# A transformer layer with retrieved experts on one core: three waits and one merge moved in the order of the engines' work

## The reference

```python
h = rmsnorm(x, g_mix);  z = h @ w_in      # pool channels | q | k | v | gate_pool | gate_attn
pool_branch = pool_mixer(p, pool_w, pool_scale) @ w_pool_out
attn_branch = gqa_attention(rope(norm(q)), rope(norm(k)), v) @ w_attn_out
x = x + (sigmoid(gate_pool) * pool_branch + sigmoid(gate_attn) * attn_branch) @ w_out
x = x + peer(rmsnorm(x, g_ffn), ...)
y = rmsnorm(x, g_final)

def peer(h):                              # for each token, 8 heads
    q = (h @ w_query).reshape(8, 2, 128)
    s = q . sub_keys                      # 2 x 128 scores a head
    sv, si = top_k(s, 16)                 # of each half
    cand = sv[0][:, None] + sv[1][None, :]            # 256 pairs, expert id = si0 * 128 + si1
    top_s, pos = top_k(cand, 16);  gate = softmax(top_s)
    a = h . expert_u[idx]                 # 128 experts a token (8 heads x 16)
    return sum(gelu(a) * gate * expert_v[idx])
```

## Time and profile before

| | before |
|---|---|
| median of 3 runs | 2856.29 us (2851.89 to 2860.07) |
| profiled execution | 2854.17 us, span of the trace 2852.4 us |
| PE busy | 2606.1 us (91%) |
| PE weight loads | 1549.7 us (54%) |
| DVE busy | 2088.7 us (73%) |
| ACT busy | 537.9 us (19%) |
| POOL busy | 1571.6 us (55%) |
| moved by DMA | 996.18 MB, 349 GB/s over the span |
| mean granted TensorE clock | 0.967 |

### The profile page before, as it was taken

One profiled execution on the slowest core, in us unless ns is written; L12 is line 12 of the kernel. 1 busy time (PEld: TensorE's weight loads), 2 busy tenths in 40 slices (PEclk: granted clock), 3 DMA queues, 4 the chain that ended last, 5 costly groups with the idle time before them and its releaser, 6 DMA issues.

```text
span 2852.4 us, 30906 instructions
## 1 busy us (share of the span) xinstructions
PE 2606.1 (91%) x9957; PEld 1549.7 (54%) x9957; DVE 2088.7 (73%) x4622; ACT 537.9 (19%) x1205; POOL 1571.6 (55%) x1284
## 2 busy tenths in 40 slices
PE   7999988989787997999589999899999999999998
PEld 6867867875234474555444455455454545444454
DVE  1232977888608876788889988977777778778786
ACT  2141151211008114544520000110000000100101
POOL 0000166456764774444267777677766667666672
PEclk9999999999999998999899999999999999999999
DMA  7538689988997897999899999999999999999994
GB/s 243 188 130 288 248 295 412 410 309 307 344 369 244 329 408 287 345 332 309 309 351 396 413 382 413 377 394 413 412 413 413 413 413 414 413 413 412 407 412 192
DMA packets 305988, 996.18 MB, mean 349 GB/s; under 512 B 26432, under 2 KB 107200, under 8 KB 276672
## 3 DMA queue, kind: packets, MB, share of 16 engines
q0 software_dynamic: 184320, 671.17, 60.9%
q1 hardware_dynamic: 69664, 292.02, 26.3%
q10 hardware_dynamic: 51872, 31.46, 3.6%
HBM read 932.68 MB, written 61.87 MB: 349 GB/s over the span
## 4 chain that ended last, share of the span: by engine, by line
PE 29%; DVE 27%; DMA 26%; issue 11%; POOL 4%; ACT 2%; another core or an unknown queue 1%; DVEq 0%; ACTq 0%; POOLq 0%; SPq 0%
DMA ring<-in_expert_v,idx 15%; PE bank L699 10%; DMA ring<-in_expert_u,idx 9%; PE bank L687 8%; DVE ring L1416 7%; PE bank L978 3%; POOL ring L1381 3%; PE o_bank L968 2%; PE o_bank L719 2%; DVE consts L1834 2%; DVE h L1416 2%; DVE consts L1828 2%; DVE region_c L1416 2%; PE bank L758 1%; DVE neg_max L1510 1%
## 5 line engine op out<-in xcount | busy, mean ns | idle before, releaser
L1381 POOL DMA_INDIRECT ring<-in_expert_u,idx x468 | 605.6, 1294 | 659.2 <-DVE idx L1719 294.2
L978 PE MATMUL bank<-wslot,gate_attn 128*128 128x512 f32 x1536 | 703.3, 609 | 54.8 <-DVE gate_attn L1768 54.7
L1381 POOL DMA_INDIRECT ring<-in_expert_v,idx x428 | 500.0, 1168 | 335.3 <-issue 113.9
L968 PE MATMUL o_bank<-region_a,wslot 128*128 128x384 f32 x2048 | 681.2, 486 | 0.0
L968 PEld LDWEIGHTS o_bank<-region_a,wslot 128*128 128x128 f32 x2048 | 389.0, 190 | 298.0 <-issue 60.3
L978 PEld LDWEIGHTS bank<-wslot,gate_attn 128*128 128x128 f32 x1536 | 296.2, 195 | 419.3 <-issue 322.8
L1416 DVE CUSTOM_DVE_ANT_0 ring<-ring,h 128x1024 f32<-128x1024 f32 x380 | 451.9, 1222 | 67.7 <-DMA ring<-in_expert_u,idx 65.2
L1433 DVE SCALAR_TENSOR_TENSOR region_b<-ring,dots,region_b 128x1024 f32<-128x1024 f32 x256 | 328.6, 1284 | 127.9 <-DMA ring<-in_expert_v,idx 111.1
L1286 ACT ACTIVATE gate_attn<-o_bank 128x384 f32<-128x384 f32 x128 | 62.7, 490 | 1279.9 <-PE o_bank L968 1270.1
L699 PE MATMUL bank<-region_b,wslot 128*128 128x256 f32 (+1 forms) x768 | 231.6, 460 | 1.6 <-ACT region_b L1015 1.6
L699 PE MATMUL bank<-region_a,wslot 128*128 128x256 f32 (+1 forms) x768 | 228.2, 455 | 1.2 <-ACT region_a L1015 1.2
(11 more groups left out here) (215 smaller groups left out, 2892.1 us busy)
## 6 DMA issues: line engine op xcount, KB each, us to landing
wslot<-in_expert_uT SPq DMA_DIRECT2D x64, 1024.0 KB
wslot<-in_expert_v SPq DMA_DIRECT2D x64, 1024.0 KB
wslot<-kept_weights SPq DMA_DIRECT2D x53, 1024.0 KB
kept_weights<-wslot SPq DMA_DIRECT2D x29, 1024.0 KB, 8.7
expert_weights<-region_p ACTq DMA_DIRECT2D x24, 1024.0 KB
wslot<-in_w_in SPq DMA_DIRECT2D x13, 1024.0 KB
region_p<-expert_weights SPq DMA_DIRECT2D x8, 1536.0 KB
region_s<-expert_weights SPq DMA_DIRECT2D x7, 1536.0 KB
```

The costliest lines, as they stand in the source:

```text
L968: ins = nc.tensor.matmul(dense_in[q][:, 0:DENSE_T], u_cols[slot][:, k, :], mergeds[1][:, k, T - DENSE_T:T], start=(k == 0), stop=(k == KD ...
L978: ins = nc.tensor.matmul(dense_out[2 * t + n][:], hidden[q][:, t * P:(t + 1) * P], v_cols[slot][:, n * 512:(n + 1) * 512], start=start, st ...
L1381: nc.gpsimd.indirect_dma_start(ring_row(n), None, expert_u if what == "u" else expert_v, bass.IndirectOffsetOnAxis(ap=ids, axis=0)).then_i ...
```

## The change

Five things are moved; no arithmetic is added or taken away.

1. SP: before the first column loads (and the reload of h2T ahead of them) it waits for job `("chosen", 2)`, the turned ids and gates of the last dense tile.
2. The fourth part of the first merge (`merge(0, 0)`, heads 6 and 7) leaves the end of group 0's `top_halves`; its steps run two at a time between the `attn_out` steps of group 1. With it, `gate_exp(0)` goes from group 1's attention to after its gates on ACT, `softmax(0)` from group 1's attention to after `norm2(1)` on DVE, and `turn_ids(g, 0)` from before `gate_attn` to after `out` on PE and to after `norm2(1)` on DVE. The dots are dealt anew: 12 become 16 ahead of `pool_out(1)`, 15 become 13 in `attn_out(1)`, 12 become 8 in `out(1)`, 8 become 10 after `norm2(1)`.
3. `out`: the number of dots at each step is a list now, and there are none ahead of the last step. In group 2, 28 become 24.
4. After `norm2(2)` the one-hots of jobs 0 and 1 come first; the last dots of the second tile (19 now, 15 before) and `weigh(1)` come after them, ahead of the one-hots of jobs 2 and 3. On ACT `gelu(1)` goes ahead of the stores of jobs 2 and 3, while `take_weights(1)` stays behind them.
5. Turned weights of the first tile: `turn_weights(2, 0)` on PE and `take_weights(0)` on ACT come after the first pool job instead of before it; the quad that was added after that job is added after the second, which has two.

```diff
@@ -1,3 +1,4 @@
+import itertools
 from contextlib import ExitStack
 
 import concourse.bass as bass
@@ -97,7 +98,7 @@
 SUM_BUFS = 4
 SUM_W = 2 * QUAD_ROWS - 1
 SEGMENTS = (
-    (0, {**{("p", c, tp): 1 for c in range(2) for tp in range(2)}, ("pooled",): 2, ("mixed",): 2,
+    (0, {("p", 0, 1): 2, ("p", 1, 0): 1, ("p", 1, 1): 1, ("pooled",): 2, ("mixed",): 2,
          **{("gate_pool", d): 2 for d in range(KD)}, **{("pool_out", d): 1 for d in range(KD)}}),
     (1, {("query", 0, 2): 1, ("query", 0, 3): 1,
          **{("query", c, step): 1 for c in range(1, KD) for step in range(4) if step != 2 or c in (2, 3, 4, 5, 6)},
@@ -120,6 +121,7 @@
 PIECE = 2
 PIECES = {2: (3, 0), 3: (0, 0), 4: (3, 2), 5: (0, 2), 6: (3, 4)}
 PARTS_AT = {2: 1, 3: 2, 0: 4, 1: 9}
+MERGE_STEPS = 2
 PARTS_SENT = {0: PEER_HEADS // PIECE - 1, EARLY: 2}
 MERGE_AT = {1: (2, PARTS_SENT[EARLY] * PIECE), 9: (3, 0), 26: (4, 0)}
 AGAIN_AT = {3: 3, 5: 4}
@@ -166,8 +168,9 @@
         yield from heads + pool + gates
     elif g == FIRST_GROUP[1]:
         yield from heads
+        yield pool[0]
         yield (g, "wT", 0), None
-        yield from pool + gates
+        yield from pool[1:] + gates
     else:
         yield from gates
     for d in range(KD):
@@ -187,8 +190,6 @@
             yield (g, "s", i + 3), None
         yield (g, "probsT", i), None
         yield (g, "probsT", i + 1), None
-    if g == LAST_GROUP[0]:
-        yield (g, "ids", 0), None
     for c in range(KD // 2):
         for d in (2 * c, 2 * c + 1):
             yield (g, "gate_attn", d), (g, "gate_attn", c)
@@ -200,6 +201,8 @@
     for c in range(D // CHUNK):
         for tp in tile_pairs(g):
             yield (g, "out", c, tp), (g, "out", c)
+    if g == LAST_GROUP[0]:
+        yield (g, "ids", 0), None
     for k in range(KD):
         yield (g, "h2T", k), None
     for c in range(HALVES // 2):
@@ -632,6 +635,7 @@
 
             for c in range(HALVES // 2 - WSLOTS, HALVES // 2):
                 filled(sp, *LAST_JOB[LAST_GROUP[1], "query", c])
+            filled(sp, LAST_GROUP[1], "chosen", len(DENSE) - 1)
             sp.wait_ge(h2t_spilled, 16)
             sp.dma_start(mergeds[1][:, :, T - DENSE_T:T - P], h2t_dram).then_inc(h2t_back, 16)
             for j in range(0, COL_SLOTS, COLS_EACH):
@@ -780,11 +784,11 @@
 
             def project_pool(g):
 
-                if g:
-                    turn_weights(g, 0)
                 for c in range(2):
                     for tp in range(2):
                         token_major((g, "p", c, tp), (g, "p", c), hTs[b], BOTH[tp])
+                        if g and (c, tp) == (0, 0):
+                            turn_weights(g, 0)
                         if g:
                             sum_rows("p", c, tp)
 
@@ -892,9 +896,6 @@
                 if g == FIRST_GROUP[1]:
                     pe.wait_ge(sums_added, 1)
                 attention(g)
-                if g == LAST_GROUP[0]:
-                    turn_ids(g, 0)
-
                 for c in range(KD // 2):
                     for d in (2 * c, 2 * c + 1):
                         feature_major((g, "gate_attn", d), (g, "gate_attn", c), hTs[b], d % 2 * P, KD)
@@ -911,6 +912,8 @@
                 for c in range(D // CHUNK):
                     for tp in tile_pairs(g):
                         token_major((g, "out", c, tp), (g, "out", c), mergeds[b], tp)
+                if g == LAST_GROUP[0]:
+                    turn_ids(g, 0)
 
                 pe.wait_ge(h2_half, TILES_BEFORE[g + 1])
                 for k in range(KD):
@@ -1082,11 +1085,12 @@
                 g = FIRST_GROUP[b]
                 if b:
                     gelu(0)
-                    take_weights(0)
-                    weigh_until(0, SUM_BUFS)
                 for c in range(2):
                     for tp in range(2):
                         move(pool_in[:, 2 * tp:2 * tp + 2, c * CHUNK:(c + 1) * CHUNK], (g, "p", c, tp), view=pair)
+                        if b and (c, tp) == (0, 0):
+                            take_weights(0)
+                            weigh_until(0, SUM_BUFS)
                         if b:
                             weigh_sums("p", c, tp)
                 if b == 0:
@@ -1142,8 +1146,8 @@
                 for i in range(0, n, 2):
                     exp(i)
                     exp(i + 1)
-                    if i == 0 and g:
-                        gate_exp(g - 1)
+                    if i == 0 and g == FIRST_GROUP[1]:
+                        gate_exp(1)
                     for ii in (i, i + 1):
                         if g:
                             moved(act, g, "s", ii)
@@ -1189,12 +1193,13 @@
 
                 def stores(c, step):
                     if g == LAST_GROUP[1]:
+                        if (c, step) == TURN_AFTER:
+                            gelu(1)
                         for n in early_weights(c, step):
                             store_weights(n)
                             if n + 2 < 2 * JOBS_PER_TILE:
                                 scale_one_hots(n + 2)
                         if (c, step) == TURN_AFTER:
-                            gelu(1)
                             take_weights(1)
                             weigh_until(1, SUM_BUFS)
                         weigh_sums("query", c, step)
@@ -1310,6 +1315,8 @@
                     gate_exp(2)
                     gate_exp(3)
                 gates(g)
+                if g == LAST_GROUP[0]:
+                    gate_exp(0)
                 if g == LAST_GROUP[1]:
                     take_chosen(0)
                 norm2(g)
@@ -1528,8 +1535,8 @@
                 for i in range(0, n, 2):
                     invert_sum(g, i)
                     invert_sum(g, i + 1)
-                    if i == 0 and g:
-                        softmax(g - 1)
+                    if i == 0 and g == FIRST_GROUP[1]:
+                        softmax(1)
                     dot(rows)
                     if i + 2 < n:
                         row_max(g, i + 2)
@@ -1547,12 +1554,12 @@
                 moved(dve, g, "attn_out", d)
                 nc.vector.tensor_tensor(merged[:, d, cols], merged[:, d, cols], a, ALU.add).then_inc(merged_ready, 1)
 
-            def attn_out(g, rows=KD * (0,)):
-                if g == LAST_GROUP[0]:
-                    turn_ids(g, 0)
+            def attn_out(g, rows=KD * (0,), piece=iter(())):
                 for d in range(KD):
                     attn_out_step(g, d)
                     dot(rows[d])
+                    for _ in zip(range(MERGE_STEPS), piece):
+                        pass
 
             def zero_sums(part):
 
@@ -1579,9 +1586,9 @@
                         if (c, tp) != (D // CHUNK - 1, tile_pairs(g)[-1]):
                             yield
 
-            def out(g, rows=0):
-                for _ in out_steps(g):
-                    dot(rows)
+            def out(g, rows=()):
+                for _, count in itertools.zip_longest(out_steps(g), rows, fillvalue=0):
+                    dot(count)
 
             def norm2(g):
                 b, tiles = GROUP_OF[g]
@@ -1871,19 +1878,24 @@
             norm2(0)
             for hp in range(HALVES):
                 top_halves(0, hp)
-                if hp % (2 * PIECE) == 2 * PIECE - 1:
+                if hp % (2 * PIECE) == 2 * PIECE - 1 and hp < HALVES - 1:
                     merge(0, 0, first=hp // 2 + 1 - PIECE, last=hp // 2 + 1)
 
-            dot(12)
+            dot(16)
             pool_out(1)
             attention(1, 1)
             dot(6)
-            attn_out(1, (3, 3, 3, 2, 2, 2, 0, 0))
+            piece = merge_steps(0, 0, PEER_HEADS - PIECE, PEER_HEADS, fine=True)
+            attn_out(1, (3, 2, 2, 2, 2, 2, 0, 0), piece)
+            for _ in piece:
+                pass
             zero_sums(0)
             dot(6)
-            out(1, 4)
+            out(1, (4, 4, 0))
             norm2(1)
-            dot(8)
+            turn_ids(1, 0)
+            softmax(0)
+            dot(10)
             for hp in range(HALVES):
                 top_halves(1, hp)
                 dot(2)
@@ -1907,16 +1919,16 @@
             zero_sums(1)
             turn_ids(2, 1)
             dot(4)
-            out(2, 4)
+            out(2, (4, 4, 4, 4, 4, 4, 0))
             norm2(2)
-            dot(EARLY * SLOTS - dotted[0])
             piece = iter(())
             for c in range(HALVES // 2):
                 for step_ in range(4):
+                    if (c, step_) == TURN_AFTER:
+                        dot(EARLY * SLOTS - dotted[0])
+                        weigh(1)
                     for n in early_weights(c, step_):
                         one_hots(n)
-                    if (c, step_) == TURN_AFTER:
-                        weigh(1)
                     if c and step_ < 2:
                         top_halves(2, 2 * c - 2 + step_)
                     if step_ == 2 and c in PIECES:
```

## The result

The changed kernel took 2839.39 us (median of 4 runs, 2833.69 to 2840.96), the kernel before 2858.18 beside it (4 runs): ratio 0.9931, 95% interval 0.9905 to 0.9957. Measured again on another chip it was 0.9954 (0.9937 to 0.9970). So 13 to 19 us are gained, where 26 were forecast.

The account below looks back on a forecast made before the run. Column loop bound by full DMA engines, its length fixed; ahead of it PE sets the pace, short of a few waits. 6 + 7.6 - 1.8 + 5.4 + 9.0 = 26.2 us off the 2856.3 median: 2830, range 2816 to 2848.

Parts of the forecast that it names:

- A: Column loads moved behind the last dense tile's turned ids (part 1): late row comes sooner, one-hots at 1371.6, 9.0 us gained.
- C: First tile's turned weights behind the first pool job (part 5): 7.6 us gained, 1.8 given back in fuller transfer stretches.
- (b): Last row of "chosen" stays late, 10 to 12 us, as ACT's store and late rows fill the queue: 2835; chance 0.10.
- (a): Full transfer stretches, 430 to 510 and 630 to 850 us, take B and C back: 2842; chance 0.18.
- B: First merge's part among attn_out steps, fewer dots in out (parts 2 and 3): 7.4 us at h2T, 6 kept.
- (c): Shorter waits also spare slow work at the lower clock, 1.4 to 2 us at four places: 2820; chance 0.13.
- (e): Part 2's steps make DVE late for the gates, out begins 5 to 8 us later: 2850; chance 0.07.
- D: One-hots ahead of the last dots after norm2(2) (part 4): turned weights at 1109.3 instead of 1114.70, 5.4 us gained.
- Its first step: In A, without SP's loads the last "chosen" row takes about 6.2 us instead of 15.03; quad starts at 1366.7.
- The second step: In A, turned ids at about 1369.5 are copied by 1370.4, and the one-hots start at 1371.6, set by DVE.
- The third step: In A, moved loads fall into 1380 to 1440, 13 us of room for 12 needed, costing nothing; without room, 12.
- (d): Slower: stalls like 5.10 us at 1317.85, perhaps engines awaiting instructions, shift onto the path; seven more give 2866; chance 0.05.

Follow-up runs that it names:

- hold_scores: Changed kernel, with GpSimd holding the first row of the second tile (row 256) until group 2's q and k are turned: ratio to before 0.9959.
- paced: Changed kernel, with ten tiny GpSimd fills, not waited for, ahead of each of rows 257 to 268: 2834.84 us, one execution.
- spaced: Changed kernel, with five waited-for GpSimd fills ahead of each of rows 257 to 267 and 509 to 519: ratio to before 0.9982.
- only_d: Kernel before with part 4 alone, out of group 2 keeping its 28 dots, so 15 stand behind the one-hots: ratio 0.9977.
- after again: Changed kernel unaltered, profiled again on another chip: ratio to before 0.9954, median 2834.65 us.
- loads_late: Changed kernel, but SP waits for weight job 84 instead of the last dense tile's turned ids before the first column loads: ratio to before 0.9996.

## Why the prediction was half right

**The range held and the forecast was 9 us low.** All of that, and more, is in A; C made up for some of it. There is luck in the number: 2839 lies between the prices of rivals (b) and (a), 2835 and 2842, and neither of their mechanisms took place. The gains below are differences of means over the traces with a part and without it.

**B was right** (forecast 6). The first column of the table is 243.5 to 247.4 us with the part moved (2.9, 3.79 and 4.81 us of waits) and 249.7 to 254.3 without: -5.9 on the means. That h2T gains more (9.6) and hT gives some back was in the steps, and the ten dots do wait for rows, as was said. Attention itself started no sooner for it, between 372 and 378 us with and without, so the 1.4 us forecast there aren't shown; the stretch behind it made up for them.

**C was undersized** (7.6 less 1.8). Leaving out `hold_scores`, `paced` and `spaced`, which alter that stretch, it is 437.0 to 443.7 us with part 5 and 447.2 to 453.6 without, -9.3. This column scatters by 7 us, and the first pair of traces alone has 3.9. The first step gave more than it was priced at (the third pool job at 630.75 against 647.57: 16.8, with 13.6 forecast), and more came back later than the 1.8 of the forecast: in that pair 11.9 us are left at h2T(2), where the forecast had 11.8 from the scores on. A part of the extra is rival (c): the job behind the turned weights takes 7.08 us at 620.17 and not 8.59, PE having waited 2.90 us and not 11.03; the granted clock is 1.00 from 620 to 627.5 us, and was 0.82 from 628 to 637. Rival (a), full stretches that take B and C back, doesn't show in the whole change; only in the trace of parts 2 and 3 alone is the second column long (453.6). Nor does (e): h2T of group 1 gained 9.6 us.

**D was a little high** (forecast 5.4, measured 3.6: 35.2 against 38.8). The wait moved as described, 7.76 us at 1094.83. The step that was passed over: four of the 19 dots had been free in `out(2)`. With 15 there, in `only_d`, the stretch is 29.7 and PE waits

```profile
1100.24 1.16 PE L758 MATMUL bank<-consts 128*128 128x128 f32 x8 [3.93 <-DVEq L1838]
```

So by this one trace part 3 in group 2 costs some 5 us of what part 4 wins, while h2T(2) has its wait of 5.24 us in both. That version in the whole change was not run.

**A was wrong: +4.7 us in the traces where -9.0 was forecast.** Its first step held. The row asked for at 1344.86 freed PE at 1351.65, 6.8 us, as against 15.03 and the 6.2 assumed. The views of the DMA queues while the row was on its way (packets, MB, share of the 16 engines' time; q1 is SP's queue, q0 GpSimd's, q10 ACT's), before (1360.46 to 1375.50) and after (1344.80 to 1351.70), show why:

```profile
q1 hardware_dynamic: 414, 2.98, 46.9%
q0 software_dynamic: 769, 2.83, 45.9%
q10 hardware_dynamic: 809, 0.41, 9.1%
```

```profile
q0 software_dynamic: 693, 2.54, 96.7%
```

The Trainium skill ("DMA: Bandwidth & Descriptors", section "Queues, rings and completion order") has each DMA engine go round between the queue rows that have work. The trace agrees: with SP's loads gone, GpSimd's share doubled and the row took about half as long. The 10 us of the prediction came from another assumption, that ACT's store takes a third of the time beside them; it took 9% and was over before the row of after was asked for.

The second step failed: "Turned ids at about 1369.5 are copied by 1370.4". In the prediction only DVE and the row were asked for what is late next. It was the signal, 8.0 us late, and GpSimd's run of gathers was what the 15 us of waiting had hidden: before, the run ended at 1372.2 and PE turned the ids at 1379.10; after, it ended at 1361.6 and PE turned them at 1355.23. So the one-hots of job 64 came at 1366.50, not at the 1354 that was to be seen (its 17.5 us of gain add up to 17.2). The third step failed as well: share 0.78 leaves 13 us of the engines, 5 MB need 12, "So they cost nothing". The average has room, but the stretch's own limit is a store that must land before ACT may go on; the jobs took 61.6 to 64.1 us instead of 57.3 to 58.7.

**Rival (d)** named the right row and the wrong cause: "another core or an unknown queue" was no engine waiting for its instructions, but, at the two places tried, a late signal of PE. The loop over the columns kept its length, to PE's last product 1403.2 us before, 1400.4 after and 1401.4 without part 1.

The parts add up to -5.9 - 9.3 - 3.6 + 4.7 = -14.1, with 13 to 19 us measured. **Open:** part 1 alone measured 7 us faster (1 to 13), against its traces and against the pair on one chip, which says 0. Twelve executions that lie 26 us apart may do that; no run settles it.

## What to carry to other kernels

Before you take away the wait that ends last, list what else is still running beneath it, not only the engine that comes next: here a run of gathers hidden under a 15 us wait became the wait. Room in a stretch is not to be read from the mean share of the DMA engines when some transfer in it gates an engine; price that transfer's delay by itself. And where executions scatter by 20 us, compare stretches between fixed places of several traces before you rank parts by their total time.

## What the hardware showed that was not expected

While GpSimd issues a run of gathers (1.24 us apart), signals of PE can arrive up to 9 us late, and then several at once. The fourteen traces agree at the turned ids of the last dense tile. In six of them (only part 1, after, after again, hold_scores, loads_late, paced) PE's last transpose ends well inside such a run, and ACT takes the ids 6.3 to 8.0 us after it. In the other eight no gather is being issued then, or one has just begun, and ACT takes them 0.04 us after it.

The whole trace of before was counted too, each signal of PE matched with the next recorded increment of its semaphore. Of 397 signals with no gather being issued in the microsecond ahead none is more than 1 us late, of the 654 others 106 are 1 to 20 us late and 33 more find no increment within 20 us (after: 0 of 384; of 667 others 130 and 42). Some of the late ones, above all the 25 (after: 32) over 9.5 us, are likely pairs badly matched, since increments are missing from the record; the zeros are not. It takes several gathers in a row: of 315 signals with at most two gathers begun in the 8 us ahead none is 1 to 9.5 us late, of 99 with six or more 45 are (after: 0 of 307, 58 of 105). In `hold_scores` the signals that can be matched are prompt from 839.5 to 847.6 us, with the run going since 838.2, and 6.6 us late or more from 849.3 to 851.0.

Full transfer queues are not the cause: from 1372.2 to 1379.9 us of the kernel before no gather is issued, the share is 1.04, and the signal of 1379.37 is there at 1379.68. A busy GpSimd is not either, for in `spaced` it fills buffers between the gathers. Stretches of the two kernels, before and after:

```profile
1372.00:1379.00 7.00, 3.26 (x16) 0.68 (x16) 0.00 (x0) 0.00 (x0) 0.18 (x1) 0.51 1.04 410
```

```profile
1356.00:1364.00 8.00, 0.13 (x1) 0.00 (x0) 0.00 (x0) 0.00 (x0) 4.31 (x5) 0.71 1.02 415
```

At 1.46 us apart the stall stays, at 3.05 it is gone (one trace each). Whether the number of gathers or their spacing decides, and what PE's signals and gathers share inside the chip, no run shows. The Trainium skill ("Perfetto Trace Analysis", section "Per-engine timelines") says that a matmul's end is estimated, and that its signal is pushed only when PSUM has acknowledged its bytes and then has to propagate, neither of which is in the profile. That agrees with a row of 0.42 us ahead of a signal 8 us late, but the page gives no figure for it. The 0.04 us of the eight traces show that neither takes long by itself.
